# A first half of a down product moved earlier in a two-layer MLP, and GpSimd's offset sums moved behind it

## What is computed

```python
m = rms_norm(h, norm_mlp_g[i])
h = h + jnp.square(jax.nn.relu(m @ w_up[i])) @ w_down[i]        # 1024 -> 4096 -> 1024
e = rms_norm(h, norm_ple_g[i])
h = h + jax.nn.sigmoid(e @ w_ple_gate[i]) * (p[i] @ w_ple_proj[i])
```

## Time and profile before

| | us |
|---|---|
| three runs, median (lowest to highest) | 2503.45 (2500.48 to 2505.54) |
| the profiled execution's own time | 2497.66 |
| its span in the profile | 2495.8 |
| PE busy in the span | 2467.5 (99%) |
| DVE, ACT, POOL busy | 1546.6, 1054.5, 135.1 |
| mean granted TensorE clock | 0.999 of full speed |

### The profile page before, as it was taken

The page is one execution under the profiler, slowest core; times in us unless marked ns, Lnnn a source line. Parts: engine busy times, 40 slices in busy tenths (PEclk is TensorE's granted clock), DMA queues, the critical chain, the costliest instruction groups (busy, mean ns, idle before and its releaser), DMA issues.

```text
span 2495.8 us, 32850 instructions
## 1 busy us (share of the span) xinstructions
PE 2467.5 (99%) x13321; PEld 2070.0 (83%) x13321; DVE 1546.6 (62%) x2134; ACT 1054.5 (42%) x1573; POOL 135.1 (5%) x161
## 2 busy tenths in 40 slices
PE   9999999999999999999999999999999999999999
PEld 7788888898997877888888998787877767899998
DVE  6556356676665745555667766667555576875655
ACT  5432234343444544223343443455553574453533
POOL 6000000000000000000000010200000000210100
PEclk9999999999999999999999999999999999999999
DMA  4122222666742221222245875322312101575843
GB/s 166 68 85 85 101 94 100 211 170 202 212 126 85 89 85 68 85 102 100 94 167 167 231 179 161 121 87 90 130 65 88 68 35 64 173 178 136 204 104 89
DMA packets 61442, 303.47 MB, mean 122 GB/s; under 512 B 6976, under 2 KB 7232, under 8 KB 40560
## 3 DMA queue, kind: packets, MB, share of 16 engines
q1 hardware_dynamic: 44208, 226.93, 25.6%
q0 software_dynamic: 12336, 45.33, 10.3%
q10 hardware_dynamic: 4752, 29.16, 3.2%
HBM read 299.28 MB, written 2.10 MB: 121 GB/s over the span
## 4 chain that ended last, share of the span: by engine, by line
PE 91%; DVE 5%; ACT 2%; issue 1%; DMA 1%; SPq 0%; ACTq 0%; DVEq 0%
PE ps L2944 36%; PE ps L3344 9%; PE ps L3305 9%; PE ps L3614 7%; PE ps L3179 6%; PE ps L2997 5%; PE ps L2971 5%; PE ps L3665 5%; PE ps L3121 2%; PE ps L3163 2%; PE ps L3143 1%; DVE w_lo L1768 1%; PE ps L3475 1%; PE ps L3491 1%; DMA raw<-weights 0%
## 5 line engine op out<-in xcount | busy, mean ns | idle before, releaser
L1768 DVE TENSOR_TENSOR w_lo<-raw,w_hi 128x2048 fp32r<-128x2048 f32 (+1 forms) x132 | 302.9, 2294 | 215.4 <-ACT w_hi L1014 165.3
L2944 PE MATMUL ps<-a_hi,w_hi 128*128 128x512 f32 x864 | 338.8, 392 | 0.3 <-DVE w_lo L1768 0.3
L2944 PE MATMUL ps<-a_hi,w_lo 128*128 128x512 f32 x864 | 336.3, 389 | 0.0
L2944 PE MATMUL ps<-a_lo,w_hi 128*128 128x512 f32 x864 | 336.2, 389 | 0.0
L1014 ACT ACTIVATE w_hi<-raw 128x2048 fp32r<-128x2048 f32 x122 | 231.4, 1896 | 167.0 <-PE ps L2944 136.1
L2944 PEld LDWEIGHTS ps<-a_hi,w_hi 128*128 128x128 f32 x864 | 162.2, 188 | 35.5 <-issue 1.5
L2944 PEld LDWEIGHTS ps<-a_lo,w_hi 128*128 128x128 f32 x864 | 162.2, 188 | 34.3 <-issue 1.0
L2944 PEld LDWEIGHTS ps<-a_hi,w_lo 128*128 128x128 f32 x864 | 162.2, 188 | 33.9
L3344 PE MATMUL ps<-a_hi,w_hi 128*128 128x512 f32 x352 | 138.7, 394 | 9.2 <-DVE a_lo L2371 6.7
L3344 PE MATMUL ps<-a_lo,w_hi 128*128 128x512 f32 x352 | 138.2, 393 | 0.0
L3344 PE MATMUL ps<-a_hi,w_lo 128*128 128x512 f32 x352 | 138.1, 392 | 0.0
(11 more groups left out here) (498 smaller groups left out, 5952.2 us busy)
## 6 DMA issues: line engine op xcount, KB each, us to landing
raw<-weights SPq DMA_DIRECT2D x133, 1024.0 KB, 4.8
raw<-weights SPq DMA_DIRECT2D x80, 512.0 KB, 4.0
ada_w<-ada ACTq DMA_DIRECT2D x24, 1024.0 KB, 4.9
sums<-weights POOLq DMA_DIRECT2D x42, 512.0 KB, 7.2
yq<-weights SPq DMA_DIRECT2D x31, 512.0 KB, 5.5
wide<-weights POOLq DMA_DIRECT2D x21, 512.0 KB, 5.7
sums<-weights SPq DMA_DIRECT2D x14, 512.0 KB, 7.3
kt<-weights SPq DMA_DIRECT2D x12, 512.0 KB, 4.2
```

The lines of the kernel that those rows point to most:

```text
L1768: dve.tensor_tensor(w_lo[n % 2][:, w], raw[n % 2][:, w], w_hi[n % 2][:, w].bitcast(F32), ALU.subtract)\
L2944: ins = pe.matmul(dst, a[i], b[j], start=done == 0, stop=done == total - 1)
```

## The change

It does four things. The last chunk gets an order of its own: (0,0) (1,0) (2,0) (0,1) (1,1) (2,1). There u = 2 uses banks 0 and 4, and waits for the two pieces that last used them instead of for the additions of u = 0. The plain unit of tiles 6 and 7 goes to banks 1 and 3, PE waits before `ple_proj` for six additions instead of four, and DVE's `ple_low(0)`, `ple_low(1)` and split of unit n0 + 8 move one job later. And POOL's offset sums wait for tile 17 of layer 1's MLP (the second tile of the plain unit, the last product before `ple_proj`) instead of for S1 of the last group.

```diff
-MLP_DOWN_JOBS = ((0, 0), (1, 0), (0, 1), (1, 1), (2, 0), (2, 1), (3, 0), (3, 1))
+MLP_DOWN_JOBS = (((0, 0), (1, 0), (0, 1), (1, 1), (2, 0), (2, 1), (3, 0), (3, 1)),) * 2 + (
+    ((0, 0), (1, 0), (2, 0), (0, 1), (1, 1), (2, 1)),)
...
+            if name in ("mlp0", "mlp1") and i >= 16:
+                b = (1, 3)[i - 16]
...
-            u, half = MLP_DOWN_JOBS[e % 8]
+            u, half = MLP_DOWN_JOBS[e // 8][e % 8]
...
-        def mlp_down_bank(u, m):
-            return ps[((5, 6), (7, 2))[u % 2][m]]
+        def mlp_down_bank(ch, u, m):
+            return ps[(0, 4)[m] if ch == u == 2 else ((5, 6), (7, 2))[u % 2][m]]
...
-            pool.wait_ge(*mlp_done(DEPTH - 1, "S1", MLP_GROUPS - 1))
+            pool.wait_ge(*tile_done(mlp_tile(DEPTH - 1, 17)))
             offsets(0, 0)
             offsets(1, 0)
...
-                        if ch == 2 and i == 2:
+                        if ch == 2 and i == 3:
                             ple_low(0)
                             ple_low(1)
                             split(n0 + 8)
...
-                    if half == 0 and u >= 2:
+                    if half == 0 and ch == u == 2:
+                        pe.wait_ge(*piece_at("four", "value", l, MLP_GROUPS - 2))
+                        pe.wait_ge(*piece_at("two", "sum", l, MLP_GROUPS - 2))
+                    elif half == 0 and u >= 2:
                         pe.wait_ge(*mlp_added(l, ch, 2 * u - 2))
...
-                pe.wait_ge(*mlp_added(l, 2, 4))
+                pe.wait_ge(*mlp_added(l, 2, 6))
```

More of the change, by code:

```diff
@@ L2375, in add_down @@
                 def add_down(ch, u):
-                    e = 8 * ch + MLP_DOWN_JOBS.index((u, 1))
+                    e = 8 * ch + MLP_DOWN_JOBS[ch].index((u, 1))
                     for m in range(2):
@@ L2380, in add_down @@
                         dve.wait_ge(*(mlp_done(l, "down", e) if m else mlp_down_done(l, ch, u)))
-                        dve.tensor_tensor(h[:, t, :], h[:, t, :], mlp_down_bank(u, m)[:, :], ALU.add)\
+                        dve.tensor_tensor(h[:, t, :], h[:, t, :], mlp_down_bank(ch, u, m)[:, :], ALU.add)\
                             .then_inc(sem("mlp_added"), 1)
@@ L2471, in _ @@
                             value("two", 2 * ch + 1)
-                        u, half = MLP_DOWN_JOBS[(e - 1) % 8] if e % 8 else (0, 0)
+                        u, half = MLP_DOWN_JOBS[ch][(e - 1) % 8] if e % 8 else (0, 0)
                         if half:
@@ L3327, in mlp_down @@
                     ch = e // 8
-                    u, half = MLP_DOWN_JOBS[e % 8]
+                    u, half = MLP_DOWN_JOBS[ch][e % 8]
                     q = MLP_JOB["down", e]
@@ L3343, in mlp_down @@
                             for a, b in ((0, 0), (0, 1), (1, 0)):
-                                ins = pe.matmul(mlp_down_bank(u, m)[:, :], w[a][:, cols], A[b][:, 4 * half + k, :],
+                                ins = pe.matmul(mlp_down_bank(ch, u, m)[:, :], w[a][:, cols], A[b][:, 4 * half + k, :],
                                                 start=half == k == a == b == 0, stop=half == 1 and k == 3 and a == 1)
```

## The result

The changed kernel takes 2485.52 us (median of four runs, 2485.10 to 2486.28) against 2501.97 us before (four runs, 2499.94 to 2505.54): a ratio of 0.9933, 95% interval 0.9916 to 0.9950. The profiled execution's own time is 2486.28, 1.0 us from the 2485.3 that the sum gave on the scale of the profiled execution of before (2497.66). So the mechanism came out step by step, and the scale on which its worth was put did not.

What follows compares the result with a forecast made beforehand. PE was busy for 99% of the span at a granted clock of 0.999, so only its stops could yield: 8.3 + 4.1 = 12.4 us off the median 2503.45 gave 2491 us, range 2486 to 2499.

Steps and rivals of the forecast that it cites:

- The three stops: PE standing before job 18 in layers 0 and 1 and job 16 in layer 1: 4.93, 3.34 and 4.11 us, together 12.4.
- rival (a): Only one part of the change pays: 2495 us, or 2495 to 2499 if (2,0) itself were late; chance 0.16.
- the spare time before (0,1): With (2,0) moved ahead, PE reaches (0,1) at 1592.81, 2.27 us after the DVE chain it waits for has ended.
- part 1: Down products (2,0) ahead of (0,1): the stop before job 18 goes in both layers, 8.3 us, bounds 6.4 to 9.9.
- the stop before job 16: Layer 1, put down to POOL's offset sums slowing DVE's low parts; moving them saves 4.1 us, bounds 2.7 to 4.4.
- What is late next: The plain unit's preparation after the later (0,1): done at 1608.2, needed at 1609.1, so hidden by at least 0.9 us.
- Bounds 0 to 2 us lost: Cost of the moved offset sums beside DVE's low part in the gate stage: taken at nothing, at most 2 us.
- (b): The stop moves along with job 18's end and POOL's sums slow the gate stage as much: 2503 us; chance 0.07.
- (c): Offset terms come too late for `lora0`, so PE stops at 1680.04: slower, 2530 us at four times the chain; chance 0.03.
- The clock behind a stop: PE at 1.2 GHz after standing some 3 us: 1.7 us lost behind each stop at most, all three 9.1 to 14.2.
- The scale: The 12.4 us read in one profiled execution were taken off the runs' median of 2503.45 us, giving 2491.
- The own-time sum: The 12.4 us taken off the profiled execution's own 2497.66 us, giving 2485.3.

Runs made afterwards that it cites:

- e1: The changed kernel with the offset sums' POOL wait put back, so the new order of down products alone: 2491.55 us, ratio 0.9957.
- e2: The kernel before with only the offset sums moved to the later place, old order of products kept: 2496.05 us, ratio 0.9978.
- e3: The kernel before with two DVE instructions swapped, piece two's low part ahead of the low part of weights three jobs ahead: 2489.36 us, ratio 0.9953.
- b1: The kernel before, unchanged, profiled once more, one execution: 2499.42 us.
- b2: The kernel before, unchanged, another single execution: 2496.92 us.
- b3: The kernel before, unchanged, ten executions: 2500.59 us, ratio 0.9998 to the kernel before beside it.
- e5: The changed kernel with the old order of the last chunk put back in layer 0 alone: 2492.16 us.
- e4: The changed kernel with the swap of two DVE instructions added, on another chip than e7: 2484.53 us.
- e6: The kernel before with the DVE swap and the offset sums moved, but the old order of products, banks and waits: 2485.48 us, ratio 0.9937.
- e7: The changed kernel with the DVE swap, the same kernel as e4, run beside the changed kernel on one chip: 2485.27 us, ratio 0.9934.

## Why the prediction was right and wrong

- **The three stops and their removal: right.** Each part took away the stops that it was said to (e1, e2), so rival (a) falls; the spare time before (0,1) was 2.26 us against 2.27 forecast, and no stop over 1 us took their place. PE's waits for `a_lo` at the down products came to 1.1 us instead of about 0.6: stops of 0.3 to 0.8 us at the ends of other chunks come and go in the unchanged copies too.
- **DVE's order as the cause of part 1: right,** and shown by e3, which changes that order alone.
- **POOL as the cause of the stop before job 16: right.** e2 moves one wait, and the stop is gone.
- **What is late next: right.** The plain unit's low part ended 4.6 us before PE needed it (at least 0.9 was given), the gate's 5.7 us (5.9), the offset terms 36 us (33). "Bounds 0 to 2 us lost" in the gate stage came out at 0.23 us on DVE, with no stop of PE there. Rivals (b) and (c) have nothing in the trace.
- **The clock behind a stop: mis-sized.** The term was "a fall of 1.7 us behind each", so 14.2 us at the most. Before job 18 of layer 1 a stop of the same length was followed by a loss of 0.1 (the first profile; none in b1 and b2 either), 1.7 (e2) and 3.0 us (b3). With 3.0 behind each of the three the upper end is 9.1 + 9.0 = 18.1, and the 16.5 measured lies inside it.
- **The scale: this step failed.** The prediction said: "the stops are the same program in all of them, so on the median's scale I forecast 2503.45 - 12.4 = 2491". The program is the same; its cost is not. Of the 12.4 us 9.1 are standing still, and 3.3 are what the clock took behind the stops in the one execution that was read. The 16.5 measured leave 7.4 for the clock and what else differs, more than the 5.1 that the range allowed with 1.7 behind each stop. In the four traces of the program the loss behind the stops was 3.4, 3.4, 1.7 and 6.8 us, so it can't be carried from one execution to the median of others. That the timed runs lost theirs behind the same stops is argued from these traces and from the kernels without the stops; the runs themselves have no timeline.
- **The 5.8 us between the profiled execution and the median** have two parts. The median of all 49 later runs is 2501.0, so 2.4 us were the draw of the three runs that gave 2503.45. The other 3.4 are about what goes with the clock: of those runs the ones at 0.999 (the profiled execution's value) and at 0.997 (the commonest) average 2498.76 and 2502.14, 3.4 us apart.
- **The own-time sum.** 2497.66 - 12.4 = 2485.3 takes the cost off the execution in which it was read, and would have been the better forecast. That it lies 0.2 us from the median measured is partly luck: the changed kernel's own profiled execution took 2486.28, and its second median was 2486.54.

The Trainium skill's page "TensorE: Matmul & The Clock Gate" (section on the HAM clock gate) says that the gate's view of PE's activity isn't tied to the kernel's own time. The traces of the same stop agree with that (0.1, 1.7 and 3.0 us lost behind it).

The spread of the runs follows the number of these stops, as far as so few runs show it: 5.1 to 7.7 us with three (the kernel before in three sittings, and b3), 6.3 with two (e2, eleven runs), 1.9 to 2.9 with one (e1, e3, e5), 0.7 to 1.6 with none (the changed kernel twice, e4, e6, e7; four or five runs each).

What stays open: why some executions also have a low stretch at 27 to 31 or 8 to 11 us from the start. It came with the change (e7) and without (b1). The traces show that a stop stands ahead of it there too, of 1.9 us or less. In b1 and in e6:

```profile
25.82 1.05 PE L3063 MATMUL ps<-consts_sb,pads 128*128 128x1 f32 x8 [1.75 <-DVE pads L1840]
...
27.75 0.63 PE L2997 MATMUL ps<-w_lo,a_hi 128*128 128x512 f32 x1
```

```profile
7.62 0.71 PE L3225 MATMUL ps<-w_hi,a_hi 128*128 128x512 f32 x1 [1.90 <-DVE a_lo L1857]
8.13 0.63 PE L3225 MATMUL ps<-w_lo,a_hi 128*128 128x512 f32 x1
```

In five traces (b1, b3, e1, e5, e7) the fall came 1.5 to 2.2 us after PE had resumed from a wait of 1.4 to 1.8 us at about 25.6; in two (e2, e6) 0.1 to 0.3 us after one of 1.9 us at 7.6 to 7.8. In the other six PE had stood 0.9 to 1.3 us at about 7.2, and its wait at about 25.6 (1.2 to 1.7 us) was followed by no fall. No run varied these waits, so the cause stays open.

## What to carry to other kernels

A stop of PE can cost more than its length: behind 3 us here 0 to 3 us more were lost at half clock, another amount in each execution. So when a change removes stops, take their cost off the very execution in which they were read, and expect the runs' spread to go with them; a profiled execution well below the median can be a sign that the clock has a part in the difference; three runs are too few to say how much. And look first at the instruction order of the engine that is waited for: one swap on DVE did the work of a new product order with new banks and waits, with less time to spare (0.2 us against 2.26).

## What was not expected of the hardware

- The same stop of 3.07 us in the same program was followed by none, one or two units of 1.71 us lost at 1.2 GHz, and once the fall came only after five matmuls at full speed (1588.57 behind a restart at 1587.26). Stops of 0.3 to 1.0 us were followed by none in any of the 13 traces, nor were those of 1.5 us before L3121 and 1.3 to 1.5 us before L3614 late in the span; near its start some of 1.4 to 1.9 us were.
- On POOL the offset sums' first load took 7.4 to 8.5 us from issue to the first sum beside the MLP's loads (six traces) and 5.5 to 5.7 us beside `ple_proj` (seven), and the first three additions 6.0 and 4.6 us. So the sums moved to the later place also became shorter as a chain, 19.7 us against 23.4.
